# One change to a fp32 transformer block on TensorE: a half-size first x block, a partial sum in the norm chain, transposes and fill products at the turns, and the SSD product moved into the next group's x job

## The chip, the cores and the metric

The kernel runs on one core of one Trainium2 chip. The metric is device time in microseconds from start to end of the program, on that core; the kernel before was run three times (2749.87, 2750.21 and 2752.62 us; median 2750.21). A further execution was recorded by the hardware profiler, and all rows below come from it.

## What is computed

One layer of a streaming encoder block in fp32, for 256 tokens of width 2048:

```
h = x + 0.5 * post(FFN1(pre(x)))                    # SwiGLU, inner width 5632; pre and post are RMS norms
u = pre(h);  proj = u @ w_in                        # pool | z | x,B,C | dt | two gates
merged = sigmoid(g_A) * poolmix(...) @ w_pool_out + sigmoid(g_B) * ssd(...) @ w_ssd_out
h = h + post(merged @ w_mix_out)
h = h + post(cross_attention(pre(h), mem))          # 4 heads, 256 memory tokens
h = h + 0.5 * post(FFN2(pre(h)))
```

The SSD branch has 8 groups of 8 heads. Per group: x and z are projected from u, x goes through a causal convolution of 4 taps and SiLU, a decay matrix per head, exp(differences of the cumulated dt * A), is multiplied by C times B (masked), and the head's output is that matrix times x * dt, plus a skip term; then it is gated by SiLU(z) and normed over the group's 512 columns.

## The kernel before

**Chunks.** Every weight matrix is read in chunks of 256 rows by 512 columns (512 KB). A job is one block of 512 output columns: 8 chunks for a contraction over 2048 ("gate", "up", "x", "z", "pin0" and so on), 22 for "down". There are 953 chunks in the order in which the jobs are planned. SyncE loads each chunk into `raw`, a ring of four. To keep fp32 precision with the fast fp32r matmul, every operand is split in a high and a low part: ScalarE copies `raw` to `wh` (line 991), VectorE subtracts to get `wl` (line 1385), and TensorE does three products per tile pair, `wh*ul`, `wh*uh` and `wl*uh`. Both other engines work three chunks ahead (`AHEAD`): `to(n)` means "split chunks until the one of number n + 2 is done". In the code of VectorE and ScalarE other work stands between such steps, in a fixed order written out by hand; each engine runs its list in order. A job in token form (`token_chunks`, lines 634 to 636) has 12 matmuls of 512 columns per chunk, one in feature form (`feature_chunks`, lines 668 to 671) 24 of 256 columns. Jobs alternate between two PSUM slots `J`; a second PSUM tensor `A` with two areas takes transposes and small products.

**Start.** SyncE loads the identity, then alternately a block of 512 columns of x and a weight chunk. TensorE turns x block 0 and block 1 (8 transposes each, line 685), then runs chunks 0 and 1, turns blocks 2 and 3 and the gain rows, and goes on. ScalarE makes `uh` (line 1048) and VectorE `ul` (line 1486) of each turned block, between the first chunks' splits; after the last block ScalarE squares all of x (line 1062) before it splits chunk 6. The row norm itself is applied behind the products, in SiLU.

**Norms behind a job by halves** (n = 1 before "pin0", n = 3 before the second FFN, n = 4 at the end). The last three chunks of the job ahead are run for the first 128 tokens (row tile 0) and then for the other 128 (`last_by_half`). ScalarE squares each half (line 1039) and takes a root (line 1010), VectorE adds up four partial sums (line 1458), scales (line 1459), multiplies by the gain row (line 1462), inverts the root (line 1470) and adds to the residual `res` in four blocks of 512 columns (line 1433): all of tile 0, then all of tile 1. TensorE turns the updated blocks (line 707): blocks 0 and 1 of both tiles, two chunks of the next job, then blocks 2 and 3.

**The SSD group loop.** A group has an x job in feature form and a z job in token form, 16 chunks, with c0 the first. VectorE's list in group i, before the change:

```
to(c0+1): finish_gate(i-1)       to(c0+3): finish_var(i-1)       to(c0+4): finish_scale(i-1)
to(c0+7): 24 operations into E (lines 1827 to 1829), seg_ready
to(c0+8): conv_in (x_in, line 1627), 4 + 3 * 4 operations of the taps (xc), one chunk split after each of the last three fours
to(c0+12): E = E * cbm (line 1838)
to(c0+14): Xdt, yb (lines 1842, 1844)        to(c0+16)
```

`finish_gate` adds the SSD product to `yb` and multiplies by SiLU(z); ScalarE then squares it, `finish_var` scales the sums, ScalarE takes the root, and `finish_scale` inverts it, scales `yb` and transposes it by 32 blocks into `y_turn`, which GpSimd moves to `yn` with 16 transfers (line 524). `y_turn` and `zs`, the SiLU(z) of the next group, share memory: ScalarE's `finish_z` waits until the move is done. TensorE turns the convolved x after z chunk 4 (line 879) and runs the SSD product, short matmuls of 64 columns (lines 888 to 890), after the z job. GpSimd also loads `csb`, the cumulated sums of the next group.

Of the kernel before, what the change touches and what calls it, by code (L numbers as in the profile page):

```python
# [19 lines left out]
ALU = mybir.AluOpType  # L20
# [6 lines left out]
P = 128  # L27
# [14 lines left out]
def hybrid_block(nc, x, mem, ffn1_pre_g, ffn1_w1, ffn1_w3, ffn1_w2, ffn1_post_g, mix_pre_g, w_in, b_gate,  # L42
# [118 lines left out]

    with ExitStack() as ctx:
# [84 lines left out]
        ssum, sv, ss, sr, ssq_res, sr_u, sr_q = (stat[:, 8 + 2 * i:10 + 2 * i] for i in range(7))  # L247

        HALF_NORMS = (1, 3, 4)
        UPDATES = {1: NJ * T, 2: NJ * T, 3: NJ * T, 4: 2 * T}  # L250
# [42 lines left out]
        x_loaded = [sem(f"x_loaded{q}") for q in range(4)]  # L293
        first_row_loaded = sem("first_row_loaded")
# [112 lines left out]
        def _(sp):  # L407
            sp.dma_start(ident[:], identity).then_inc(ident_loaded, 16)

# [87 lines left out]
            for n in range(2 * T):  # L497

                t, c = n // 2, slice(n % 2 * D // 2, (n % 2 + 1) * D // 2)
                sp.wait_ge(res_ready, updates_before(4) + n + 1)  # L500
                sp.dma_start(out[0, t * P:(t + 1) * P, c], res[:, t, c]).then_inc(stored, 16)
            sp.wait_ge(stored, 16 * 2 * T)
# [3 lines left out]
        def _(pool):  # L506
# [38 lines left out]

            for n, g in enumerate((mix_pre_g, xattn_pre_g, ffn2_pre_g, mem_norm_g, pool_scale)):
                pool.dma_start(rows[(n + 1) * KD:(n + 2) * KD, 0, :], g[0].rearrange("(b p) -> b p", p=P)).then_inc(rows_loaded, 16)
# [59 lines left out]
        def _(pe):  # L607
# [71 lines left out]

            def turn(k, src):  # L680
# [17 lines left out]
            def turn_halves(n, qs):  # L698

                for t in range(T):  # L700
                    for q in qs:
                        pe.wait_ge(res_ready, updates_before(n) + NJ * t + q + 1)
                        if t == 0:
                            claim_area(q % 2, (f"pre{n}", q))
                        for m in range(M):
                            c = slice(q * NCOL + m * P, q * NCOL + (m + 1) * P)
                            tr = nc.tensor.transpose(area(q % 2)[:, m, t * P:(t + 1) * P], res[:, t, c], ident[:])
                        if t == T - 1:
                            tr.then_inc(t_ready[q % 2], 1)
# [17 lines left out]
            def ffn(f):  # L727
# [6 lines left out]
                def pair(i=None):  # L734
# [3 lines left out]
                    if i is None and f == 1:  # L738
                        turn_halves(n, (0, 1))
                    before = pre_wait(n) if i is None else None  # L740
                    token_chunks(("gate", f, 0), uh, ul, range(0, 2), CD - 1, i, 2 * CD, before)
                    if i is None:
                        (turn_res if f == 0 else turn_halves)(n, (2, 3))
                        if f == 0:
                            turn_rows()
                    token_chunks(("gate", f, 0), uh, ul, range(2, CD), CD - 1, i, 2 * CD, before)
# [36 lines left out]
            turn_halves(1, (0, 1))  # L783
            feature_chunks("pin0", uh, ul, range(0, 2), CD - 1, before=pre_wait(1))
            turn_halves(1, (2, 3))
            feature_chunks("pin0", uh, ul, range(2, 7), CD - 1, before=pre_wait(1))
# [72 lines left out]

            def group(i=None):  # L860
                chunk[0] = first(("x", 0))
                per = 2 * CD
                claim(("x", 0), i)
                if i is None:
                    feature_chunks(("x", 0), uh, ul, range(0, 5), CD - 1, i, per)
# [3 lines left out]
                else:  # L869
                    feature_chunks(("x", 0), uh, ul, range(0, 6), CD - 1, i, per)  # L870
                feature_chunks(("x", 0), uh, ul, range(6, CD), CD - 1, i, per)
                claim(("z", 0), i)
                token_chunks(("z", 0), uh, ul, range(0, 5), CD - 1, i, per)
# [7 lines left out]
                token_chunks(("z", 0), uh, ul, range(5, CD), CD - 1, i, per)  # L881

                pe.wait_ge(w_ready, lin(1, i, 1))
                pe.wait_ge(xdt_ready, lin(1, i, 1))
                claim_area(1, ("Y", 0), i)
                for h in range(HPG):
                    c = slice(h * HEAD_DIM, (h + 1) * HEAD_DIM)
                    nc.tensor.matmul(A[:, 1, 0, c], E[:, h, 0:P], Xdt[:, 0, c], start=True, stop=True)  # L888
                    nc.tensor.matmul(A[:, 1, 1, c], E[:, h, P:2 * P], Xdt[:, 0, c], start=True, stop=False)  # L889
                    mm = nc.tensor.matmul(A[:, 1, 1, c], E[:, h, 2 * P:3 * P], Xdt[:, 1, c], start=False, stop=True)  # L890
                mm.then_inc(t_ready[1], 1)
# [5 lines left out]
            for j in range(NJ):  # L897
                claim(("gate_b", j))
                token_chunks(("gate_b", j), uh, ul, range(CD), CD - 1)
# [77 lines left out]
        def _(act):  # L977
            at_chunk = [0]
            act.dma_start(rows[0:KD, 0, :], ffn1_pre_g[0].rearrange("(b p) -> b p", p=P)).then_inc(first_row_loaded, 16)
# [48 lines left out]
            def last_squares(name):  # L1028
# [987 lines left out]
```

## Time and profile before

| | us |
|---|---|
| median of three runs | 2750.21 |
| the profiled execution | 2751.63 |
| its span, first to last instruction | 2750.0 |
| TensorE busy | 2719.7 |
| VectorE busy | 1633.9 |
| ScalarE busy | 1288.3 |
| GpSimd busy | 346.4 |

The span is what the engines' rows cover. "Busy" of TensorE includes overlap of pipelined matmuls, so a busy engine can still be slower than it could be. "Granted clock" is a share of TensorE's full 2.4 GHz. In a timeline row "x4" means that four instructions of a kind are merged; the brackets give the idle time of the engine before the row and what ended it. In the chain of waits a row is a piece of the chain that ended last.

### The profile page before, as it was taken

The numbers are of one execution on the slowest core, as the hardware profiler recorded it, in microseconds if no ns is written. First come the engines' busy times: TensorE is split into PE (matmuls) and PEld (weight loads), VectorE is DVE, ScalarE is ACT, GpSimd is POOL, SyncE is SP. The second block draws the span as 40 slices with busy tenths as digits, with TensorE's granted clock in tenths as the row PEclk, the third lists the DMA queues.
The fourth block names the chain that finished last, engine by engine and source line by source line (L and its number), as shares of the span: only waits on it lengthen the run. The fifth ranks groups of instructions, "written<-read, shape, count | busy, mean of one in ns | idle before, by whom it ended". The sixth has DMA issues, their size and how long they took to land.

```text
span 2750.0 us, 39291 instructions
## 1 busy us (share of the span) xinstructions
PE 2719.7 (99%) x13990; PEld 2331.4 (85%) x13990; DVE 1633.9 (59%) x1912; ACT 1288.3 (47%) x1442; POOL 346.4 (13%) x619
## 2 busy tenths in 40 slices
PE   8999999999999999999999999999999999999998
PEld 7888888888899889989989888888978888888887
DVE  5555555444577556787887765566565555554444
ACT  5444444444454544455555564445654444444443
POOL 1121212000000000011311201223002122120000
PEclk9999999999999999999999999999999999999999
DMA  7777767666566665566666666677457676676554
GB/s 223 210 206 201 211 199 210 196 198 198 164 183 192 206 200 181 171 195 189 190 198 184 191 204 200 202 232 228 164 162 209 201 205 206 205 210 199 196 197 160
DMA packets 286209, 541.46 MB, mean 197 GB/s; under 512 B 27456, under 2 KB 27840, under 8 KB 285856
## 3 DMA queue, kind: packets, MB, share of 16 engines
q1 hardware_dynamic: 263104, 504.07, 59.7%
q0 software_dynamic: 22976, 36.07, 4.8%
q8 instruction: 64, 1.05, 0.1%
q14 instruction: 33, 0.27, 0.0%
q10 hardware_dynamic: 32, 0.01, 0.0%
HBM read 519.53 MB, written 2.16 MB: 190 GB/s over the span
## 4 chain that ended last, share of the span: by engine, by line
PE 94%; DVE 4%; ACT 1%; issue 1%; DMA 1%; DVEq 0%; SPq 0%; ACTq 0%
PE J L634 25%; PE J L636 25%; PE J L635 25%; PE J L668 5%; PE J L671 5%; PE J L670 5%; DVE wl L1385 1%; PE A L890 1%; PE A L889 1%; PE A L888 1%; ACT wh L991 0%; DVE E L1828 0%; DMA raw<-in_w_mix_out_dram 0%; DVE E L1829 0%; PE A L685 0%
## 5 line engine op out<-in xcount | busy, mean ns | idle before, releaser
L1385 DVE TENSOR_TENSOR wl<-raw,wh 128x1024 fp32r<-128x1024 f32 x950 | 1155.3, 1223 | 977.7 <-ACT wh L991 971.1
L991 ACT ACTIVATE wh<-raw 128x1024 fp32r<-128x1024 f32 x950 | 1004.0, 1060 | 1269.4 <-PE J L636 1017.0
L634 PE MATMUL J<-wh,ul 128*128 128x512 f32 x2048 | 801.9, 392 | 7.7 <-DVE wl L1385 4.9
L635 PE MATMUL J<-wh,uh 128*128 128x512 f32 x2048 | 798.9, 390 | 0.0
L636 PE MATMUL J<-wl,uh 128*128 128x512 f32 x2048 | 798.8, 390 | 0.0
L634 PEld LDWEIGHTS J<-wh,ul 128*128 128x128 f32 x2048 | 385.7, 188 | 94.1 <-issue 12.7
L636 PEld LDWEIGHTS J<-wl,uh 128*128 128x128 f32 x2048 | 385.6, 188 | 80.7
L635 PEld LDWEIGHTS J<-wh,uh 128*128 128x128 f32 x2048 | 385.8, 188 | 79.0
L668 PE MATMUL J<-ul,wh 128*128 128x256 f32 x1088 | 310.5, 285 | 2.0 <-DVE ul L1486 2.0
L671 PE MATMUL J<-uh,wl 128*128 128x256 f32 x1088 | 308.8, 284 | 0.0
L670 PE MATMUL J<-uh,wh 128*128 128x256 f32 x1088 | 308.8, 284 | 0.0
L517 POOL DMA_DIRECT2D hraw<-turned x320 | 173.2, 550 | 752.9 <-DVE turned L1527 746.5
L634 PE MATMUL J<-wh,hidl 128*128 128x512 f32 x680 | 264.7, 389 | 0.0
L636 PE MATMUL J<-wl,hidh 128*128 128x512 f32 x680 | 264.5, 389 | 0.0
L635 PE MATMUL J<-wh,hidh 128*128 128x512 f32 x680 | 264.5, 389 | 0.0
L668 PEld LDWEIGHTS J<-ul,wh 128*128 128x128 f32 x1088 | 209.8, 193 | 2.5 <-DVE ul L1486 2.2
L670 PEld LDWEIGHTS J<-uh,wh 128*128 128x128 f32 x1088 | 209.8, 193 | 0.1
L671 PEld LDWEIGHTS J<-uh,wl 128*128 128x128 f32 x1088 | 209.7, 193 | 0.0
L635 PEld LDWEIGHTS J<-wh,hidh 128*128 128x128 f32 x680 | 127.7, 188 | 26.6
L634 PEld LDWEIGHTS J<-wh,hidl 128*128 128x128 f32 x680 | 127.7, 188 | 26.4
L636 PEld LDWEIGHTS J<-wl,hidh 128*128 128x128 f32 x680 | 127.7, 188 | 26.3
L524 POOL DMA_DIRECT2D yn<-y_turn x128 | 74.7, 592 | 284.0 <-DVE y_turn L1527 283.6
(273 smaller groups left out, 2173.6 us busy)
## 6 DMA issues: line engine op xcount, KB each, us to landing
raw<-in_ffn_w_dram SPq DMA_DIRECT2D x528, 512.0 KB, 4.4
raw<-in_w_in_dram SPq DMA_DIRECT2D x257, 512.0 KB, 3.8
raw<-in_w_ssd_out_dram SPq DMA_DIRECT2D x64, 512.0 KB, 3.6
raw<-in_w_pool_out_dram SPq DMA_DIRECT2D x32, 512.0 KB, 4.1
raw<-in_w_mix_out_dram SPq DMA_DIRECT2D x32, 512.0 KB, 6.0
hraw<-turned POOLq DMA_DIRECT2D x320, 32.0 KB, 4.0
csb<-cs_dram POOLq DMA_DIRECT2D x16, 512.0 KB, 6.3
raw<-in_pool_w_dram SPq DMA_DIRECT2D x8, 512.0 KB, 5.0
```

The source lines that it names most:

```text
L517: pool.dma_start(dst[32 * c:32 * (c + 1), :, a * 64:(a + 1) * 64], src[32 * a:32 * (a + 1), c].rearrange("p k t n -> p k (t n)")).then_inc ...
L524: pool.dma_start(dst[32 * c:32 * (c + 1)].rearrange("p k (t a n) -> p (k t) a n", t=T, n=32)[:, :, a], src[32 * a:32 * (a + 1), c].rearran ...
L634: nc.tensor.matmul(o[:, t], b, wh[:, r, kk], start=(k == 0 and kk == 0), stop=False)
L635: nc.tensor.matmul(o[:, t], a, wh[:, r, kk], start=False, stop=False)
L636: mm = nc.tensor.matmul(o[:, t], a, wl[:, r, kk], start=False, stop=(k == last_k and kk == CK - 1))
L668: nc.tensor.matmul(o[:, m], h, b, start=(k == 0 and kk == 0 and m % 2 == 0), stop=False, skip_group_check=True)
L670: nc.tensor.matmul(o[:, m], h, a, start=False, stop=False, skip_group_check=True)
L671: mm = nc.tensor.matmul(o[:, m], l, a, start=False, stop=(k == last_k and kk == CK - 1), skip_group_check=True)
L888: nc.tensor.matmul(A[:, 1, 0, c], E[:, h, 0:P], Xdt[:, 0, c], start=True, stop=True)
L889: nc.tensor.matmul(A[:, 1, 1, c], E[:, h, P:2 * P], Xdt[:, 0, c], start=True, stop=False)
L991: nc.scalar.activation(wh[:, r], raw[:, r], ACT.Copy).then_inc(high, 1)
L1385: nc.vector.tensor_tensor(wl[:, r], raw[:, r], wh[:, r].bitcast(F32), ALU.subtract).then_inc(low, 1)
```

## The change

1. **x load.** SyncE loads the first 256 columns of x, chunk 0, the other 256 columns of block 0, chunk 1, block 1, chunk 2, chunk 3, block 2, chunk 4, block 3. The identity is loaded from ScalarE's queue. GpSimd's nine loads of gain and convolution rows wait for the second half block.
2. **Start on TensorE.** 16 products of a constant, 4 and 10 products of the identity are run ahead of and around the first transposes. Chunks 0 to 3 are run pass by pass (`pass_chunk`: all `high`, all `low_x`, all `low_w` matmuls), with the second half of block 0 turned after chunk 0, block 1 after chunk 1, block 2 after chunk 2, block 3 and the rows after chunk 3.
3. **Norm chain.** VectorE adds the first three partial sums ahead (`partial`); ScalarE adds the last one inside the root. Tile 0's last block is updated after tile 1's first two (n = 3), or after its gain product (n = 1); VectorE splits and TensorE turns in a changed order (`after_halves`) with 8 and 5 products of the identity between; at the end row tile 1 is stored in four parts.
4. **SSD.** The product of group i - 1 is run after chunk 4 of group i's x job (and of the first "gate_b" job), and VectorE's and ScalarE's pieces move with it. The move of `yn` is awaited block by block.

The core of the diff, in the order of this list (VectorE's `post_halves` and `group`, then ScalarE's `group`, stand last):

```diff
         def _(act):
             at_chunk = [0]
+            act.dma_start(ident[:], identity).then_inc(ident_loaded, 16)
...
         def _(sp):
-            sp.dma_start(ident[:], identity).then_inc(ident_loaded, 16)
...
             def load_x(k):
-                if k < 4:
-                    c = slice(k * NCOL, (k + 1) * NCOL)
-                    sp.dma_start(res[:, :, c], x[0].rearrange("(t p) d -> p t d", p=P)[:, :, c]).then_inc(x_loaded[k], 16)
+                xs = x[0].rearrange("(t p) d -> p t d", p=P)
+                if k == 0:
+                    c = slice(0, NCOL // 2)
+                    sp.dma_start(res[:, :, c], xs[:, :, c]).then_inc(x_first, 16)
+                elif k in (1, 2, 4, 5):
+                    q = {1: 0, 2: 1, 4: 2, 5: 3}[k]
+                    c = slice(q * NCOL + (NCOL // 2 if q == 0 else 0), (q + 1) * NCOL)
+                    sp.dma_start(res[:, :, c], xs[:, :, c]).then_inc(x_loaded[q], 16)
...
+            def after_halves(name, n, feature=False):
+                idle = J[:, slot(name), 1, 0:P]
+                turn_half(n, 0, 0)
+                turn_half(n, 0, 1)
+                fill(idle, ident, 8)
+                turn_half(n, 1, 0)
+                fill(idle, ident, 5)
+                pass_chunk(name, n, 0, W_FIRST, feature, after_first=lambda: turn_half(n, 1, 1))
+                pass_chunk(name, n, 1, X_FIRST, feature)
+                for q in (2, 3):
+                    for t in range(T):
+                        turn_half(n, t, q)
+                pass_chunk(name, n, 2, X_FIRST, feature)
+                pass_chunk(name, n, 3, X_FIRST, feature)
...
+                    if i is None and f == 0:
+                        pass_chunk(("gate", f, 0), n, 0, X_FIRST)
+                        turn_x_half(1)
+                        pass_chunk(("gate", f, 0), n, 1, X_FIRST)
+                        turn_res(n, (1,))
+                        pass_chunk(("gate", f, 0), n, 2, X_FIRST)
+                        turn_res(n, (2,))
+                        pass_chunk(("gate", f, 0), n, 3, X_FIRST)
+                        turn_res(n, (3,))
+                        turn_rows()
...
+            pe.wait_ge(fill_ready, 1)
+            fill(J[:, 1, 1, 0:P], ones, 16)
             pe.wait_ge(ident_loaded, 16)
-            turn_res(0, (0,))
             pe.wait_ge(first_row_loaded, 16)
             nc.tensor.transpose(J[:, 0, 0, 0:KD], rows[0:KD, 0, :], ident[0:KD, 0:KD]).then_inc(cols_ready, 1)
-            turn_res(0, (1,))
+            fill(J[:, 1, 1, 0:P], ident, 4)
+            turn_x_half(0)
+            fill(J[:, 1, 1, 0:P], ident, 10)
...
+                for t in range(T):
+                    dve.wait_ge(half_squares, T * HALF_NORMS.index(n) + t + 1)
...
+                    elif t == 0:
+                        inverse(t)
+                        for q in range(NJ - 1):
+                            quarter(0, q)
+                        gain(t)
+                        for q in range(NJ - 1, T0_FIRST[n]):
+                            quarter(0, q)
+                    else:
+                        inverse(t)
+                        quarter(1, 0)
+                        quarter(1, 1)
+                        lows(0)
+                        advance()
+                        for q in range(T0_FIRST[n], NJ):
+                            quarter(0, q)
+                        quarter(1, 2)
+                        gain(t)
+                        lows(1)
+                        advance()
+                        quarter(1, 3)
...
                 else:
                     to(c0 + 1, i, per)
-                    finish_gate(0, i - 1)
-                    to(c0 + 3, i, per)
-                    finish_var(0, i - 1)
-                    to(c0 + 4, i, per)
-                    finish_scale(0, i - 1)
+                    scale_x(0, i - 1)
+                    to(c0 + 2, i, per)
+                    weigh(slice(HPG // 2, HPG), 0, i - 1).then_inc(w_ready, 1)
+                    to(c0 + 6, i, per)
+                    finish_gate(0, i - 1)
...
                 l.then_inc(seg_ready, 1)
                 to(c0 + CD, i, per)
-                conv(("x", 0), xc, 0, i, per, M)
-                to(c0 + CD + 4, i, per)
-                dve.wait_ge(exp_ready, lin(1, i, 1))
-                nc.vector.tensor_tensor(E[:], E[:], c.to_broadcast([P, HPG, 3 * P]), ALU.mult).then_inc(w_ready, 1)
+                if i is not None:
+                    finish_var(0, i - 1)
+                conv_in(("x", 0), i, per)
+                if i is not None:
+                    finish_scale(0, i - 1)
+                conv_taps(("x", 0), xc, 0, i, per, M)
                 to(c0 + CD + 6, i, per)
+                weigh(slice(0, HPG // 2), 0, i)
...
                 to(c0 + CD, i, per)
                 if i is not None:
                     root(g_root + 1, i - 1)
...
                 nc.scalar.activation(E[:], E[:], ACT.Exp).then_inc(exp_ready, 1)
-                to(c0 + CD + 4, i, per)
+                to(c0 + CD + 6, i, per)
                 conv_silu(("x", 0), xc[:], xc_silu, i)
-                to(c0 + CD + 6, i, per)
+                to(c0 + 2 * CD, i, per)
```

`scale_x` holds the two operations that make `Xdt` and `yb`, `weigh` half of `E` times `cbm`.

## Rows read from the trace of the kernel before

**Rows 1.** The page, part 1: busy time of each engine.
```profile
PE 2719.7 (99%) x13990; PEld 2331.4 (85%) x13990; DVE 1633.9 (59%) x1912; ACT 1288.3 (47%) x1442; POOL 346.4 (13%) x619
```

**Rows 2.** Waits of TensorE: total us, times, longest us.
```profile
PE A L685 <- DMA res<-in_x_dram: 8.0, 2, 6.5
PE J L634 <- DVE wl L1385: 4.9, 9, 1.0
```

**Rows 3.** Busy time by stretch, 17 to 728 us: PE, PEld, DVE, ACT, POOL; clock.
```profile
17.00:728.00 711.00, 711.00 (x3152) 589.12 (x3150) 367.04 (x338) 313.53 (x332) 88.74 (x164) 1.00 0.68 202
```

**Rows 4.** Timeline of the start: TensorE, then ScalarE (start, us, operation).
```profile
12.92 0.76 PE L634 MATMUL J<-wh,ul 128*128 128x512 f32 x1 [0.82 <-issue]
...
16.89 0.43 PE L634 MATMUL J<-wh,ul 128*128 128x512 f32 x1
...
9.90 1.55 ACT L1048 ACTIVATE uh<-A,cols 128x256 fp32r<-128x256 f32 x4
...
26.20 1.96 ACT L1062 ACTIVATE F<-res 128x2048 f32<-128x2048 f32 x1
...
30.48 2.94 ACT L991 ACTIVATE wh<-raw 128x1024 fp32r<-128x1024 f32 x3
...
39.33 1.27 ACT L1090 ACTIVATE silu_g<-J,stat 128x512 f32<-128x512 f32 x2 [0.30 <-PE J L636]
```

**Rows 5.** Chain of waits around norm 1 (start, us, what).
```profile
736.64 0.70 ACT J L1039 x2
...
738.54 0.76 DVE res L1433
...
742.62 0.58 PE J L668
...
750.74 1.75 PE A L707 x16
...
766.88 0.43 PE A L790 x2
```

**Rows 6.** Timeline around norm 3: TensorE.
```profile
2014.20 1.97 PE L707 MATMUL A<-ident,res 128*128 128x128 f32 x8 [2.56 <-DVE res L1433]
2017.94 0.80 PE L634 MATMUL J<-wh,ul 128*128 128x512 f32 x1 [1.77 <-DVE ul L1486]
...
2039.38 0.47 PE L634 MATMUL J<-wh,ul 128*128 128x512 f32 x1 [0.18 <-DVE wl L1385]
```

**Rows 7.** Busy time and clock (PEclk) by stretch: norms and group loop.
```profile
740.50:741.00 0.50, 0.17 (x2) 0.00 (x0) 0.20 (x2) 0.50 (x3) 0.00 (x0) 0.60 0.31 90
...
2013.00:2014.00 1.00, 0.00 (x0) 0.00 (x0) 0.87 (x3) 1.00 (x2) 0.00 (x0) 0.89 0.02 8
...
1319.00:1555.00 236.00, 233.34 (x1517) 210.92 (x1516) 192.41 (x313) 127.32 (x132) 46.91 (x76) 1.00 0.63 188
```

**Rows 8.** Timeline of a group of the SSD loop: VectorE, TensorE, GpSimd.
```profile
1210.44 1.23 DVE L1385 TENSOR_TENSOR wl<-raw,wh 128x1024 fp32r<-128x1024 f32 x1 [1.65 <-ACT wh L991]
...
1222.89 1.23 DVE L1385 TENSOR_TENSOR wl<-raw,wh 128x1024 fp32r<-128x1024 f32 x1
...
1244.57 1.22 DVE L1771 TENSOR_TENSOR yb<-A,yb 128x1024 f32<-128x1024 f32 x1 [1.71 <-PE A L890]
...
1255.49 0.16 DVE L1782 RECIPROCAL stat<-stat 128x2 f32<-128x2 f32 x1
...
1257.83 1.18 DVE L1385 TENSOR_TENSOR wl<-raw,wh 128x1024 fp32r<-128x1024 f32 x1
...
1214.91 0.40 PE L634 MATMUL J<-wh,ul 128*128 128x512 f32 x1
...
1224.27 0.47 PE L634 MATMUL J<-wh,ul 128*128 128x512 f32 x1 [1.00 <-DVE wl L1385]
...
1239.07 0.33 PE L888 MATMUL A<-Xdt,E 128*128 128x64 f32 x2
...
1205.66 9.36 POOL L524 DMA_DIRECT2D yn<-y_turn  x16 [38.59 <-DVE y_turn L1527]
```

More of the change, by code:

```diff
@@ L737, in pair @@
                     n = {0: 0, 1: 3}[f]
-                    if i is None and f == 1:
-                        turn_halves(n, (0, 1))
                     before = pre_wait(n) if i is None else None
[L741 to L746, printed above, removed]
+                    if i is None and f == 0:
[8 more added lines that the diff above has]
+                        turn_rows()
+                    elif i is None:
+                        after_halves(("gate", f, 0), n)
+                    done_ks = 0 if i is not None else 4
+                    token_chunks(("gate", f, 0), uh, ul, range(done_ks, CD), CD - 1, i, 2 * CD, before)
                     if i is None and f == 0:
@@ L782, in _ @@
             claim("pin0")
[L783 to L786, printed above, removed]
+            after_halves("pin0", 1, feature=True)
+            feature_chunks("pin0", uh, ul, range(4, 7), CD - 1, before=pre_wait(1))
             pe.wait_ge(normed, 2)
@@ L858, in _, with ssd @@
             feature_job("C1")
+            def ssd(i=None):
+                pe.wait_ge(w_ready, lin(GROUPS, i, 1) if i is None else i)
+                pe.wait_ge(xdt_ready, lin(GROUPS, i, 1) if i is None else i)
+                pe.wait_ge(t_moved[1], use(1, ("Y", GROUPS - 1)) - 1 if i is None else lin(use(1, ("Y", 0)) - 2, i, 1))
+                for h in range(HPG):
+                    c = slice(h * HEAD_DIM, (h + 1) * HEAD_DIM)
+                    nc.tensor.matmul(A[:, 1, 0, c], E[:, h, 0:P], Xdt[:, 0, c], start=True, stop=True)
+                    nc.tensor.matmul(A[:, 1, 1, c], E[:, h, P:2 * P], Xdt[:, 0, c], start=True, stop=False)
+                    mm = nc.tensor.matmul(A[:, 1, 1, c], E[:, h, 2 * P:3 * P], Xdt[:, 1, c], start=False, stop=True)
+                mm.then_inc(t_ready[1], 1)
             def group(i=None):
@@ L880, in group @@
                 tr.then_inc(t_ready[0], 1)
[L881 to L891, printed above, removed]
+                token_chunks(("z", 0), uh, ul, range(7, CD), CD - 1, i, per)
             group()
@@ L1502, in pre_norm_behind @@
                 if n == 0:
-                    for q in range(2):
-                        first_splits(q)
-                        pre_low(n, q)
+                    pre_low(n, 0, range(0, 2))
+                    first_splits(0)
+                    pre_low(n, 0, range(2, M))
+                    first_splits(1)
+                    pre_low(n, 1)
                     first_splits(2)
@@ L1582, in _ @@
             ffn(0)
-            post_halves(1, ("down", 0, NJ - 1), 0.5, between=lambda q: pre_low(1, q))
+            post_halves(1, ("down", 0, NJ - 1), 0.5, lows=lambda q: pre_low(1, q))
             nc.vector.memset(ones[:], 1.0)
```

245 lines of the change are left out of this document (168 added, 77 removed).

## The prediction

> **What bounds the kernel now.** I read the page first: TensorE is busy for 2719.7 of 2750.0 us [rows 1], so a change can win only its idle time, its time at half clock, or fewer instructions; this one keeps the arithmetic. Then TensorE's waits [rows 2]: 8.0 us for x at the start and 4.9 us for `wl`, one time in each pass of the group loop. From 17 to 728 us there is no idle at all: 3152 matmuls in 711.00 us, so 0.2256 us each and 2.71 us for a chunk of 12 [rows 3]. What is left lies in four places, read as timelines: the start [rows 4], the norm before "pin0" [rows 5], the norm before the second FFN [rows 6] and the SSD group loop [rows 8]. The last view carries the most weight: it shows what precedes the one wait of each group.
>
> **Base.** The profiled execution took 2751.63 us with a span of 2750.0; the median of the runs is 2750.21. I sum changes against the profile and put them on the median.
>
> **The start.** Now the first chunk begins at 12.92, late and at half clock (full from 16.89), but afterwards TensorE never idles, and the first gate job ends where SiLU begins, 39.3 [rows 4]. After: 30 tiny matmuls fill the wait. Eight transposes at half clock take 1.97 us [rows 6], 0.21 each start to start; if the engine starts at 1.4 (assumed), 16 fills end at 4.8, the row transpose and 4 fills at 5.9, four half-block transposes at 6.8. The x half lands somewhere between 1.4 and 6.5 (the full block today, TensorE's longest wait for it [rows 2]); below 5.9 it does not matter. ScalarE then makes two `uh` (0.8) and `wh` 0 (1.0; three take 2.94) [rows 4], to 8.8. Chunk 0 starts at 8.9, 4 us earlier than now, and at full clock ends at 11.7.
>
> From there the new order costs. The second half is turned only behind chunk 0 (to 12.3); ScalarE makes `uh` 2, 3 and then `wh` 1 (1.8 us), so chunk 1 starts at 14.3: 2.0 us idle. x block 1 is turned only behind chunk 1 (to 18.0); ScalarE makes four `uh` (1.55) and then `wh` 2 (1.0), so chunk 2 starts at 20.7: 2.7 us idle. Chunks 2 and 3 and the turns behind them run to 28.3. The last block is turned at 28.0, so its `uh` end at 29.6, `wh` 5 at 30.7, and the two squares with the root (26.20 to 30.48 now, 4.3 us) let `wh` 6 start at 34.9 against 30.48 now. Chunk 5 waits 0.8 us and chunk 6 2.5 us for `wl`; chunk 7 ends near 42.8 against 39.2. **Start: +3.6 us**, between -4 (if ScalarE's queue did not hold up the turns, the 4 us of the earlier start stay won) and +7 (if the clock falls in the 2.7 us gap). I take +3.6: every wait in it is an engine's own order. Moved DMAs: `ident` goes to ScalarE's queue ahead of the gain row (one issue, behind the fills); GpSimd's nine row loads queue behind the wait for x block 0 (about 8), a half us of issue each, needed at 27.9; the last x block is issued behind `w` 4, which waits for `wl` 0 (about 10), and is needed at 27. All at nothing. If rows came after 28, every us would count.
>
> **Norm 1.** Now the second row tile is turned behind its first update, from 739.3, the first chunk starts at 742.62, and by the matmul of `diag`, 766.88, seven chunks are done [rows 5]. Added: a reduce and two scalings ahead of the last squares, under the last matmuls. Removed behind each square: a reduce, a scaling, and the gain product's place ahead of the reciprocal. The square ends at 737.3; root and reciprocal (0.2 us each) now end in 738.54, then in 737.9. An update takes 0.76, so the second tile's blocks are ready at 738.6 and 739.3 against 739.3 and 740. Turn, two `uh`, first pass: `uh` from 739.4, chunk 0 at 740.35. That is 2.3 us earlier, with the q1 turn inside the chunk, and without half clock: now the clock falls at 740.6 [rows 7], while the 13 fills leave gaps of 0.7 us only. A feature chunk is 2.88 us (752.5 to 766.88 are five); chunks 0 and 1 with the q1 turn end at 746.5. The block (1, 3) is updated after `lows(1)` and one `wl`, at 748.0, so turns end at 748.5 (1.0 us of wait, new). Five more chunks end at 762.95; `wh` 6, behind the squares, is ready at 758.3 and `wl` 6 at 759.5, 0.5 us before its use. **-3.9 us**, between -5 and -1 (without the clock's part).
>
> **Norm 3.** The same for token chunks. Now the second tile's work waits for VectorE's four first-tile updates, turns at 2014.20, chunk 0 at 2017.94, then at half clock (0.80 us for the first matmul), and chunk 6 starts at 2039.38 [rows 6, 7], so the job ends at 2044.8. After: only three first-tile updates come first, 0.68 for the product, reciprocal at 2011.7, turn at 2012.7, chunk 0 at 2014.3; chunk 1 ends at 2020.2; block (1, 3) comes at 2022.6 (1.2 us of wait); six chunks from 2023.15 end at 2039.5. **-5.3 us**, between -6.5 and -2.
>
> **The end.** The last updates are four for two, at best as fast; the reduce and the scaling behind the last square go, and the last store is half as large. **-0.2**, between -0.5 and +0.3.
>
> **The SSD loop.** The 48 short matmuls are moved and not removed: they start at 1239.07, VectorE takes their result at 1244.57 [rows 8], and TensorE has no wait among its rows for their inputs. So moving them gains nothing by itself. VectorE's order changes. With z starting at 1214.91 (its fourth chunk is the one that waits), `wl` 9 comes at 1210.44, bound to `wh` 9 and so to x chunk 5; then 24 `E`, `wl` 10, `x_in`, four taps, four taps, and `wl` 11 at 1222.89, in which VectorE idles only 0.4 us. TensorE needs `wl` 11 about 1223.1 and starts at 1224.27: 1.2 us lost per group, seven times (group 0 alike). The change takes out of that stretch nothing; `E` times `cbm`, `Xdt` and `yb` (some 5.8 us in all) stood behind it. It puts in `finish_var` (0.1) and `finish_scale`, which from reciprocal to next instruction runs 1255.49 to 1257.83, 2.34 us. `finish_gate` (2.45) moves to c0 + 6, under the 5.3 us of short matmuls, done 0.2 us before chunk 5 is, so `wl` 9 is no earlier. `wl` 11 is 2.44 us later, the wait 3.6 us. **7 x 2.44 = +17.1 us**, between 0 (if the stretch began earlier) and +23 (3.3 each). Else in the loop: ScalarE's root waits behind `wl` 10 with `Exp` and three `wh` queued behind it; `Exp` ends 7 us into z and `wh` 11 at 8, VectorE asks for it at 10.3: covered. GpSimd's `yn` move starts 6.4 us into z and takes 9.4 us to issue [rows 8], with the last landing perhaps 13 to 14; its end is awaited by ScalarE's `finish_z` 26 us into z, 6 us of slack; if it took twice as long each group would pay 7. The `E` product's second half, `Xdt` and `yb` (4.1 us) in the next x job end 5 us before the short matmuls. After the loop everything has a chunk or more of slack.
>
> **The clock in the loop.** The clock fell to 1.2 GHz at 740.6 and at 2013.9; before each fall TensorE had idled but for eight or some transposes [rows 5 to 7]. In the loop, idle times of 1.0 us never lower it [rows 7]. The new 3.4 us of idle lie between the two, nearer the first. At the start a rise took dense matmuls from 12.92 to 16.89, 4.0 us [rows 4], at 0.43 us each instead of 0.23: 1.9 us lost. I take three falls in seven groups: **+6 us**, between 0 and +20. The Trainium skill's TensorE: Matmul & The Clock Gate ("What's actually happening") says the clock is lowered only after a whole idle window; by it these gaps, with dense matmuls on both sides, would almost never lower it and the sum would be 6 us smaller.
>
> **Sum.** 3.6 - 3.9 - 5.3 - 0.2 + 17.1 + 6 = +17.3; on the median 2767.5, rounded down to **2767.0**.
>
> **Rivals.**
> (a) The same without falls of the clock in the loop: +11.3, 2761.5. For it: only gaps that held a few transposes or nothing, and were longer or began with slower work, have lowered it so far.
> (b) The other side: VectorE's stretch starts early enough, or `finish_scale` hides, so that the loop's wait does not grow. Place: between `x_in` and the first taps. The loop then costs 0 and the edges decide: -5.8, 2744.4; 2736 if today's 1.2 us go as well. It decides as soon as the growth per group is under 5.8 / 7 = 0.8 us. Against it: 0.4 us of idle in the stretch, and its start hangs on x chunk 5, which the change leaves where it is relative to z.
> (c) The clock falls in every group and in the start's gap, or the `yn` move is late too: +21 to +29, 2771 to 2779.
> (d) The half block brings nothing because it lands as late as the whole one: the start +0.7 more. Inside the range of each.
>
> **Chances.** Forecast 0.42, (a) 0.28, (b) 0.16, (c) 0.09, and 0.05 for the edges and the loop near zero together. A measurement here tells 0.2%, 5.5 us, from no change. Slower by more: 0.79 (forecast, (a), (c)); faster by more: (b) where its -5.8 or -14 hold, 0.13; within: 0.08. The range takes the forecast and (a) with their edges' bounds and most of (c): 2753 to 2778.
>
> **What would show it.** TensorE's wait of `J` for `wl` at about 3.4 us, once per group, total near 24 us, with `yb` and `y_turn` between `x_in` and `xc` on VectorE; in the start, waits for `wh` of 2.0 and 2.7 us and the first SiLU near 43; first chunk near 9; chunk 0 of "pin0" 4 us after the last FFN matmul at full clock; granted clock below 1.00 in some groups. It would be wrong if the group's period stayed near 52 us instead of 54.6, or the first SiLU came before 39.

## The result and the profile after

The changed kernel takes **2768.11 us** (median, 2766.0 to 2771.38), the kernel before 2751.80 us beside it (2749.87 to 2754.55): the ratio is 1.0061 with a 95% interval of 1.0049 to 1.0072. It is slower by 16.3 us; 2767.0 was forecast, and a change of +17.3 on a median of 2750.21, which became 2751.80 with two more runs. The profiled execution has a span of 2766.6 us against 2750.0, so the spans differ by 16.6. The page, part 1, and under it TensorE's costliest group of part 5:

```profile
PE 2730.8 (99%) x14102; PEld 2343.3 (85%) x14102; DVE 1633.1 (59%) x1920; ACT 1287.9 (47%) x1442; POOL 345.2 (12%) x619
...
L660 PE MATMUL J<-wh,ul 128*128 128x512 f32 x2016 | 789.5, 392 | 22.0 <-DVE wl L1505 21.9
```

TensorE is busy 11.1 us longer than in [rows 1], though it gained only 112 records. The new matmuls are the constant products (fills) at the turns, and the same matmuls take longer where the clock is low. The waits of TensorE (total us, times, longest) say where the idle time is:

```profile
PE J L660 <- DVE wl L1505: 21.9, 11, 2.7
PE J L737 <- ACT wh L1104: 4.5, 2, 2.6
PE J L709 <- DVE ones L1737: 1.2, 1, 1.2
PE A L771 <- DVE res L1553: 0.7, 1, 0.7
```

The 8.0 us for x [rows 2] are gone, and 4.5 us for `wh` at the start came in their place. The wait for `wl` grew from 4.9 to 21.9 us, with 18.4 of it in seven times in the loop, where it was 4.3 before, and 2.7 in two chunks at the start. To see what each part of the change did, I took the same operation in both traces and compared its start, in order of time:

```
mark (TensorE)                           before      after    part        its share
turn of hidden behind the first job      501.53     508.28    start          +6.7
first turn of norm 1                     736.44     743.18
diag matmul behind norm 1                766.71     769.84    norm 1         -3.6
first turn of merged, behind the loop   1826.45    1848.90    loop          +19.3
first turn of norm 3                    2010.36    2032.84
last matmul                             2742.02    2759.23    norm 3         -5.3
end of the span                          2750.0     2766.6    end            -0.6
```

The shares make +16.6 with rounding, the difference of the spans. What follows goes through them in this order.

**The start**, TensorE (start, duration, operation, idle time before it):

```profile
1.19 5.53 PE L709 MATMUL J<-ones 128*128 128x128 f32 x32 [1.19 <-DVE ones L1737]
...
10.40 1.17 PE L737 MATMUL J<-wh,uh 128*128 128x512 f32 x4
...
15.72 1.23 PE L737 MATMUL J<-wh,uh 128*128 128x512 f32 x4 [1.87 <-ACT wh L1104]
...
22.27 2.08 PE L737 MATMUL J<-wh,uh 128*128 128x512 f32 x4 [2.60 <-ACT wh L1104]
24.14 1.60 PE L737 MATMUL J<-wh,ul 128*128 128x512 f32 x4
25.59 1.08 PE L737 MATMUL J<-wl,uh 128*128 128x512 f32 x4
```

The first chunk starts at 10.40 instead of 12.92 [rows 4] and at full clock, but chunks 1 and 2 each wait for their `wh`. Chunk 2 then runs at half clock for its first pass and most of its second (2.08 and 1.60 us where chunk 1 has 1.23 and 1.09). ScalarE's first SiLU shows what the job has lost: 46.31 against 39.33 [rows 4].

```profile
19.71 1.57 ACT L1161 ACTIVATE uh<-A,cols 128x256 fp32r<-128x256 f32 x4 [4.04 <-PE A L751]
21.15 1.07 ACT L1104 ACTIVATE wh<-raw 128x1024 fp32r<-128x1024 f32 x1
...
46.31 1.26 ACT L1212 ACTIVATE silu_g<-J,stat 128x512 f32<-128x512 f32 x2
```

ScalarE stood idle 4.04 us until TensorE, which had chunk 1 to do first, turned the next block. Then it split that block and the weights while TensorE stood idle. The two engines take turns instead of overlapping.

The +6.7 is one execution's. Six of the experiments below (e1, e3, e4, e7, e8, e9) have the same start, and their turn of hidden lies between 506.52 (e3) and 509.63 (e1), so between +5.0 and +8.1. In e3 the 16 fills took 5.24 us, chunk 0 came at 10.11 and the clock did not fall behind it; in e1 they took 6.72 us, chunk 0 came at 11.59 and the clock fell.

**Norm 3** (norm 1 has the same form), TensorE:

```profile
2032.84 1.04 PE L771 MATMUL A<-ident,res 128*128 128x128 f32 x8
2033.72 1.95 PE L709 MATMUL J<-ident 128*128 128x128 f32 x16
...
2037.15 1.16 PE L737 MATMUL J<-wh,uh 128*128 128x512 f32 x4
...
2045.30 0.66 PE L771 MATMUL A<-ident,res 128*128 128x128 f32 x4 [0.65 <-DVE res L1553]
```

From the first turn to chunk 0 it is 4.31 us, against 7.58 before (2010.36 in the table to 2017.94, [rows 6]). The chunk runs at full clock: its first four matmuls take 1.16 us, where the first one alone took 0.80.

**The loop**, the chain of waits of one group (start, us, what):

```profile
1330.74 1.14 DVE wl L1505
...
1331.95 1.14 DVE x_in L1786
...
1333.40 0.89 DVE yb L1943 x2
...
1335.18 0.37 issue
1335.55 1.38 DVE xc L1800 x4
```

It ends in a `wl` at 1338.86 and a matmul of TensorE at 1340.24, after 2.60 us of idle time. The two scalings of `yb` and the turn `y_turn` lie between `x_in` and `xc`. By the timelines of VectorE `xc` begins 3.7 us behind `x_in`, and 1.5 us before the change. Before, then after:

```profile
1217.43 1.21 DVE L1627 TENSOR_TENSOR x_in<-J,rbc 128x1024 f32<-128x1024 f32 x1
1218.92 2.02 DVE L1641 TENSOR_SCALAR xc<-x_in,cols 128x256 f32<-128x256 f32 x4 [0.28 <-DVE x_in L1627]
```

```profile
1213.58 1.23 DVE L1505 TENSOR_TENSOR wl<-raw,wh 128x1024 fp32r<-128x1024 f32 x1 [1.44 <-ACT wh L1092]
...
1220.63 1.21 DVE L1786 TENSOR_TENSOR x_in<-J,rbc 128x1024 f32<-128x1024 f32 x1
...
1224.32 1.37 DVE L1800 TENSOR_SCALAR xc<-x_in,cols 128x256 f32<-128x256 f32 x4
```

The `wl` at 1213.58 is the one ahead of the 24 `E`, and the matmul that waits starts at 1229.12. I call these 15.5 us the stretch.

From one turn of `xc` to the next it is 54.2 us in three groups and 55.3 to 55.7 in four; it was 52.1 on average before (1230.02 to 1542.68 in six). The longer ones are those in which the clock fell. Two pieces of 3.4 us behind the wait, one with a fall and one without (columns as in [rows 7]; the clock is the third number from the end):

```profile
1229.10:1232.50 3.40, 3.38 (x10) 2.74 (x11) 3.28 (x7) 0.00 (x0) 3.40 (x7) 0.66 0.71 196
1340.20:1343.60 3.40, 3.36 (x14) 2.60 (x15) 3.28 (x7) 0.00 (x0) 3.40 (x7) 1.00 0.73 191
```

The waits ahead of them are almost equal, 2.72 and 2.60 us. Over the loop's seven waits the clock fell four times, each time for 3.4 us at 1.2 GHz.

### The profile page after: what moved, and what is told of

It is laid out like the page before. It is cut to its first block, busy times and chain, and to the rows that moved or that the text cites. A ratio compares the mean times of both kernels' runs of the same rounds, so it can differ in the third digit from the quotient of the medians.

```text
span 2766.6 us, 39541 instructions
## 1 busy us (share of the span) xinstructions
PE 2730.8 (99%) x14102; PEld 2343.3 (85%) x14102; DVE 1633.1 (59%) x1920; ACT 1287.9 (47%) x1442; POOL 345.2 (12%) x619
## 4 chain that ended last, share of the span: by engine, by line
PE 94%; DVE 4%; ACT 1%; issue 1%; DMA 0%; DVEq 0%; ACTq 0%
PE J L660 25%; PE J L662 25%; PE J L661 25%; PE J L694 5%; PE J L697 5%; PE J L696 5%; DVE wl L1505 1%; PE J L737 1%; PE A L963 1%; PE A L962 1%; PE A L961 1%; PE J L709 0%; PE J L733 0%; ACT wh L1092 0%; DMA raw<-in_w_mix_out_dram 0%
## 5 line engine op out<-in xcount | busy, mean ns | idle before, releaser
L660 PE MATMUL J<-wh,ul 128*128 128x512 f32 x2016 | 789.5, 392 | 22.0 <-DVE wl L1505 21.9
L661 PE MATMUL J<-wh,uh 128*128 128x512 f32 x2016 | 786.8, 390 | 0.0
L662 PE MATMUL J<-wl,uh 128*128 128x512 f32 x2016 | 786.8, 390 | 0.0
L660 PEld LDWEIGHTS J<-wh,ul 128*128 128x128 f32 x2016 | 380.0, 188 | 106.3 <-ACT wh L1092 21.8
L662 PEld LDWEIGHTS J<-wl,uh 128*128 128x128 f32 x2016 | 379.8, 188 | 79.5
L694 PE MATMUL J<-ul,wh 128*128 128x256 f32 x1056 | 300.2, 284 | 0.0
L697 PE MATMUL J<-uh,wl 128*128 128x256 f32 x1056 | 298.8, 283 | 0.0
L696 PE MATMUL J<-uh,wh 128*128 128x256 f32 x1056 | 298.8, 283 | 0.0
L694 PEld LDWEIGHTS J<-ul,wh 128*128 128x128 f32 x1056 | 202.6, 192 | 0.5
L696 PEld LDWEIGHTS J<-uh,wh 128*128 128x128 f32 x1056 | 202.6, 192 | 0.3
L697 PEld LDWEIGHTS J<-uh,wl 128*128 128x128 f32 x1056 | 202.6, 192 | 0.0
```

The lines of the kernel that those rows point to most:

```text
L660: nc.tensor.matmul(o[:, t], b, wh[:, r, kk], start=(k == 0 and kk == 0), stop=False)
L661: nc.tensor.matmul(o[:, t], a, wh[:, r, kk], start=False, stop=False)
L662: mm = nc.tensor.matmul(o[:, t], a, wl[:, r, kk], start=False, stop=(k == last_k and kk == CK - 1))
L694: nc.tensor.matmul(o[:, m], h, b, start=(k == 0 and kk == 0 and m % 2 == 0), stop=False, skip_group_check=True)
L696: nc.tensor.matmul(o[:, m], h, a, start=False, stop=False, skip_group_check=True)
L697: mm = nc.tensor.matmul(o[:, m], l, a, start=False, stop=(k == last_k and kk == CK - 1), skip_group_check=True)
```

## The experiments

The kernel before took 2752.50 us beside e1 to e8 (13 runs, 2751.04 to 2754.55) and 2751.61 beside e9 and e10 (15 runs, 2749.47 to 2753.42). In the traces I read the mean period of the loop from the turns of `xc`. Each of e2 to e8 is one run; their differences are to be held against the 3.5 us over which the 13 runs of the kernel before spread.

**e1: the change without its loop.** All hunks of the diff stay, but the 48 short matmuls stand behind z again and the finish of `y` in front of the 24 `E`, as before. From TensorE's part:

```
-                    ssd(i)
-                    feature_chunks(("x", 0), uh, ul, range(5, 6), CD - 1, i, per)
+                    feature_chunks(("x", 0), uh, ul, range(0, 6), CD - 1, i, per)
```

> The changed kernel with its group loop put back as it was; start and norms stay changed. Theory (VectorE's order in the loop costs 2.1 us a group, and 1.2 us for each fall of the clock, 19.3 us by the marks of the two traces): the loop's period returns from 54.2 or 55.4 to 52.1 us, TensorE's waits for wl in it to at most 1.0 us, no fall of the clock in it, time 2768.1 - 19.3 = 2748.8 us (ratio to the kernel before 0.9989). Rival (the loop is only where time lost at the norms or the start shows up): the loop would keep a period over 53 us and the time would stay above 2755.

2749.68 us (2747.09 to 2750.8), ratio 0.9988 with an interval of 0.9978 to 0.9997. The period is 52.2 us and the clock in the loop is 1.00. The other parts of the change together win 2.8 us by the medians, as their marks said (6.7 - 3.6 - 5.3 - 0.6); in the profiled execution of e1, the slowest of its ten runs, it is 0.9 us, because its start is +8.1. The loop alone turned that into a loss.

**e2: the loop alone.** The reverse: the kernel before with only the loop's hunks.

> The kernel before with the changed group loop alone. Theory: the mirror of the run above, 2751.8 + 19.3 = 2771 us, between 2766.5 (no fall of the clock) and 2775 (a fall in each of seven groups); waits for wl of 2.7 us, seven times. Rival (the loop costs only together with the changed start or norms): 2752.

2772.87 us, one run: +20.4, with a period of 55.1 and four falls of the clock in the loop, the first of them twice as long (6.8 us). Together, e1 and e2 give -2.8 + 20.4 = +17.6, and the whole change +16.3: the parts add up to about 1 us, so none of them causes or hides much of another.

**e3: the stretch 0.8 us shorter.** This leaves out the two scalings of `yb` in groups 0 to 6, so what they computed is missing from the result.

```
-                for t in range(T):
-                    l = nc.vector.tensor_scalar(yb[:, t], yb[:, t], sr[:, t:t + 1], None, ALU.mult)
-                l.then_inc(y_normed, 1)
+                if i is None:
+                    ...
+                else:
+                    dve.sem_inc(y_normed, 1)
```

> The changed kernel; in the loop the two scalings of yb by the inverse root (0.44 us each) are left out, so groups 0 to 6 are not normed. Theory (every us that VectorE works between x_in and the first taps is a us of TensorE's wait): the wait falls from 2.7 to 1.8 us, the period from 54.2 to 53.3, 6.2 us in seven groups, and with less idle time the clock falls in 0 to 2 groups instead of 4 (2.4 to 4.8 us more): 2757 to 2760. Rival (the place of the SSD product in the x job costs, not VectorE's list): 2768, the period unchanged.

2756.04 us, the period 53.4 or 53.5 in every group. The wait shrank from 2.6 to 1.8 or 1.9 us, and the clock fell in no group. The waits of TensorE in the loop (1200 to 1570 us), the changed kernel and then e3:

```profile
PE J L660 <- DVE wl L1505: 18.4, 7, 2.7
```

```profile
PE J L660 <- DVE wl L1505: 12.8, 7, 1.9
```

The time lies 1 us below the range that I expected. The start of this execution was 1.8 us shorter than the changed kernel's (506.52 against 508.28), which has nothing to do with the edit.

**e4: the stretch 0.8 us longer.** Two more scalings, with `zs` as their output, ahead of the two.

```
+                if i is not None:
+                    for t in range(T):
+                        nc.vector.tensor_scalar(zs[:, t], yb[:, t], sr[:, t:t + 1], None, ALU.mult)
```

> The changed kernel; in the loop the two scalings of yb are run a second time into a spare tile (0.9 us more). Theory: the wait grows from 2.7 to 3.6 us, 6.2 us in seven groups, and the clock falls in 5 to 7 groups (1.2 to 3.6 us more): 2775.5 to 2778. Rival (VectorE's list is not what the loop waits for): 2768.

2778.88 us, 0.9 above the range that I expected. The same view of e4:

```profile
PE J L660 <- DVE wl L1505: 23.8, 7, 3.4
```

The period is 56.2 to 56.4 where the clock fell for 3.4 us, 57.6 where it fell for 6.8, and 55.0 in the one group of seven where it did not fall. So from e3 over the changed kernel to e4 the wait goes 1.8, 2.6, 3.4 with the length of the stretch, and the falls 0, 4, 6. The whole stretch, from the `wl` ahead of the 24 `E` to the matmul that waits, is 13.2 to 13.8 us before the change, 14.6 or 14.7 in e3, 15.4 or 15.5 in the changed kernel and 16.2 in e4, and in every group of the four the wait is the stretch less 12.8 us. These 12.8 us are what VectorE has; what it takes beyond them TensorE waits for. Both terms that I forecast for the loop are shown here: VectorE's stretch sets the wait one for one, and the clock is an extra on top that comes more often with a longer wait.

**e5 and e6: another order at the start.** Both are e1 with the second half of x block 0 turned behind the first, five fills fewer, and each further block turned one chunk earlier; e6 also starts the split of chunk 6's weights ahead of the squares.

```
+            turn_x_half(1)
-            fill(J[:, 1, 1, 0:P], ident, 10)
+            fill(J[:, 1, 1, 0:P], ident, 5)
...
                         pass_chunk(("gate", f, 0), n, 0, X_FIRST)
-                        turn_x_half(1)
-                        pass_chunk(("gate", f, 0), n, 1, X_FIRST)
                         turn_res(n, (1,))
-                        pass_chunk(("gate", f, 0), n, 2, X_FIRST)
+                        pass_chunk(("gate", f, 0), n, 1, X_FIRST)
...
```

> As e1_loop_as_before (old loop, changed norms), with the start's order changed: x's second half is turned ahead of chunk 0 in place of five of the ten fills, block 1 behind chunk 0, block 2 behind chunk 1, block 3 behind chunk 2. Theory (in the changed start TensorE waits for ScalarE because each block is turned one chunk too late; the row of waits for wh, 4.5 us, the 2.7 us of waits for wl behind it and the half clock of 3.4 us go): the first gate job ends near 36.5 instead of 45.8 us, time 2749.7 - 9.3 = 2740.4 us. Rival (x has not landed so early, so the waits for wh turn into waits for x): the gate job ends above 43 and the time stays above 2747.

> As e5_start_turns_early, and ScalarE and VectorE split chunk 6 before the squares of x and the root. Theory: chunk 6 waits for wl 0.5 to 1 us at most in e5, so this gains 0 to 1 us: 2739.5 to 2740.5. Rival (the squares still set the start, as they did in the changed kernel with 1.9 us): it gains 2 us or more against e5, 2738.

2742.99 and 2742.45 us: 9.5 and 10.1 us under the kernel before and 6.7 and 7.2 under e1. The 0.5 between the two is less than single runs can tell. TensorE in e6, from chunk 0 on:

```profile
11.65 1.16 PE L737 MATMUL J<-wh,uh 128*128 128x512 f32 x4 [0.43 <-issue]
...
15.26 1.17 PE L737 MATMUL J<-wh,uh 128*128 128x512 f32 x4
...
18.87 1.17 PE L737 MATMUL J<-wh,uh 128*128 128x512 f32 x4
```

Chunk 0 starts no later than in e1 (11.65 against 11.59; 10.40 in the changed kernel, whose fills were over sooner), nothing waits behind it any more, and the clock does not fall; the first SiLU comes at 37.13. The turn of hidden is at 499.34 against 509.63 in e1, 10.3 us earlier. Of these, 1.9 are given back behind the loop: one load of `w_mix_out` took 11.91 us there (10.06 in e1), its chunk came late, and TensorE waited up to 2.2 us for it, in e5 up to 2.4. The spans differ by the 8.4 that are left (2749.1 and 2740.7). This late load is most of the 2 to 3 us by which both lie above what I expected.

**e7: the norms without fills.** e1 without the two groups of constant products in `after_halves`.

```
                 turn_half(n, 0, 1)
-                fill(idle, ident, 8)
                 turn_half(n, 1, 0)
-                fill(idle, ident, 5)
```

> As e1_loop_as_before, without the 8 and 5 fill products in the two norms by halves. Theory A (the fills keep the clock up; the gain of the norms is half the reordering and half the clock): the clock falls at one or both norms and 1.2 to 3 us each are lost, 2752 to 2755. Theory B (the reordering alone leaves gaps too short for a fall): no fall, and since the fills end before the turned blocks are ready, the same time within 0.7 us: 2749.7.

2750.41 us, 0.7 above e1's median and within its runs. TensorE at norm 1 (idle time in brackets):

```profile
746.60 0.66 PE L771 MATMUL A<-ident,res 128*128 128x128 f32 x4 [1.34 <-DVE res L1547]
748.27 1.19 PE L733 MATMUL J<-uh,wh 128*128 128x256 f32 x8 [1.02 <-ACT uh L1153]
```

Two gaps of 1.3 and 1.0 us did not lower the clock, nor did the 1.6 and 1.0 us at norm 3. In the new order of the norm the fills do nothing for the time; what wins it is the rest, the order and the partial sum, which no run separates.

**e8: the scalings behind the taps.** The changed kernel, with `finish_scale` after the first convolution taps instead of before them.

```
+                conv_taps(("x", 0), xc, 0, i, per, M)
                 if i is not None:
                     finish_scale(0, i - 1)
-                conv_taps(("x", 0), xc, 0, i, per, M)
```

> The changed kernel with finish_scale moved from between x_in and the taps to behind the taps. Theory (the wait for wl is VectorE's list; but the move of yn then starts some 10 us later and ScalarE's finish_z, which needs it done, waits): the waits for wl 11 fall to 1.0 us and the clock falls vanish, 19.3 us less, while finish_z comes 5 to 7 us late and the fourth x chunk waits 1 to 2.5 us for its wl, 7 to 17 us back: 2756 to 2766. Rival (the yn move has slack enough): 2749.

2780.39 us: slower than the changed kernel, where I had expected it to be faster. The chain of waits says why (start, us, what):

```profile
1234.01 0.89 DVE yb L1943 x2
...
1236.53 8.62 POOL yn L549 x15
1245.15 5.17 DMA yn<-y_turn
...
1251.04 0.68 ACT zs L1335
1251.72 0.95 ACT wh L1092
...
1256.32 1.24 DVE wl L1505
1257.69 0.36 PE J L694
```

The wait in z did shrink, to 1.00 us. But `y_turn` now ends near 1236 instead of 1224, GpSimd needs 8.6 us to issue its 16 moves, and the last of them lands at 1250.3. ScalarE's `zs` waits for that (6.98 us idle), with the splits of the weights queued behind it, and TensorE then waits in the next x job:

```profile
PE J L694 <- DVE wl L1505: 11.6, 9, 2.1
PE J L660 <- DVE wl L1505: 9.5, 13, 1.0
```

In the changed kernel the same `zs` at 1245.68 is released by TensorE and not by the moves. This is the mechanism of my rival (c), the late `yn` move, and I had put 6 us of slack on it in the prediction. A delay of 12 us uses that up and more. The expectation named this wait and took 7 to 17 us for it, which was much too little: from the `diag` matmul to the first turn of merged it is 10.8 us more than in the changed kernel, where I had expected 2 to 12 less. One reason is that the clock went on falling. It fell at 1310.5, 1368.5, 1481.2 and 1593.8, each time within 1.4 us behind the end of one of the new waits, of 1.9 to 2.5 us. The rest of the difference is not worked out.

**e9: the stretch begins earlier, in the changed kernel.** The first 12 of the 24 `E` tiles may be written one chunk earlier; the work stays the same.

```
-                else:
-                    to(c0 + 7, i, per)
...
-                    if i is None and h == HPG // 2 - 1:
-                        to(c0 + 7)
+                    if h == HPG // 2 - 1:
+                        to(c0 + 7, i, per)
```

> The changed kernel; the one edit is that VectorE may write the first 12 of a group's 24 E tiles one chunk earlier (from chunk 6 of the x job), in the time in which it stood idle ahead of the low product of wl. In the profile of the changed kernel VectorE stood idle 1.44 us at that place (1213.58, behind ACT wh) and then had no idle time until the low product that TensorE waited 2.72 us for (1229.12). If the unbroken stretch of VectorE work sets that wait, it begins up to 1.44 us earlier, the wait falls to about 1.3 us, the four falls of the clock in the loop (1.2 us each, behind gaps of 2.6 to 2.7 us) go too, and the time falls by 7 x 1.4 + 4 x 1.2 = 14.6 us to about 2753.5 us, wl waits of TensorE from 21.9 to about 12 us. If the wait comes from the order of the taps and low products alone, or from the transfers of the weights, nothing moves: 2768 us.

2753.14 us (2752.06 to 2753.64, ten runs), ratio to the kernel before 1.0006 with an interval of 0.9996 to 1.0015. The period is 52.7, and the clock stays up in every group. This one edit of an order takes back 15.0 us of what the change lost. It shows that the place of VectorE's work, not its amount, sets the time: by the waits it took 1.5 us out of each group, about as much as VectorE had stood idle ahead of the stretch (1.44 us), and with the shorter waits the four falls went too. TensorE's waits in the loop:

```profile
PE J L660 <- DVE wl L1505: 5.4, 5, 1.1
PE J L660 <- ACT wh L1092: 2.3, 2, 1.2
```

**e10: the same edit on e6.** The norms of the change, the start of e6, and the loop as before with the halved `E`.

> The kernel of e6 (the norms of the change, its start with the turns one chunk earlier, the loop as before), with one edit: the first 12 of the 24 E tiles may be written from chunk 6 of the x job instead of chunk 7. In the profile of e6 TensorE waited for wl 4.6 us in the loop, 7 times, longest 1.0, and VectorE stood idle 1.65 us just ahead of the stretch that ends in that wait. If the stretch sets the wait, all 4.6 us go: 2742.5 - 4.6 = about 2738 us, and no wait of TensorE on wl is left in the loop. If something else sets it: 2742.5 us with the waits unchanged. The work on either engine is the same in both.

**2731.73 us** (2730.99 to 2732.15), ratio 0.9927 with an interval of 0.9913 to 0.9941: 19.9 us under the kernel before and 36.4 under the changed one. Busy time by stretch (TensorE first), e6 and then e10:

```profile
1100.00:1500.00 400.00, 395.63 (x2691) 364.03 (x2690) 319.91 (x535) 205.02 (x210) 68.72 (x110) 1.00 0.64 188
```

```profile
1100.00:1500.00 400.00, 399.87 (x2750) 372.07 (x2749) 322.12 (x537) 209.48 (x217) 68.91 (x110) 1.00 0.62 190
```

TensorE's idle time in the loop is gone. It gave 10.7 us where I expected 4.6; by the spans it is 10.2, of which 8.2 lie ahead of the first turn of merged and 2.1 behind it. The 2.1 are the late load of e6, which took 9.91 us here. The 8.2 are the loop, whose period went from 52.2 to 51.1 us. The wait rows understate a gap: the modelled end of a matmul lies 0.16 us past the start of the next one, so the gap of 0.43 us at 1217.92 in e6 cost 0.59, and the first matmul behind it 0.07 more. Over seven gaps that is 1.6 of the 3.6 us between 4.6 and 8.2. Another 1.3 lie one chunk later, where no gap is listed: in each group of e6 the next chunk's first matmul starts 0.31 to 0.35 us behind the one before it instead of 0.23, and the matmul behind it is 0.08 late again (1220.53, 1220.84 and 1221.15 in the first of the seven). The last 0.7 are open; e6 has one run only.

## Why the prediction was right

**The start, +3.6 forecast, +6.7 measured.** The mechanism held: every wait in my list is there. `wh` 1 and `wh` 2 release the first two (1.87 and 2.60 us, forecast 2.0 and 2.7), `wl` 5 and `wl` 6 the other two (0.87 and 1.87, forecast 0.8 and 2.5). Two sizes were off. I took 0.21 us for a fill, from the eight transposes at half clock in [rows 6]. A 128-column product of these is two records, and 16 of them took 5.53 us, so 0.34 us each, and chunk 0 came at 10.40 instead of 8.9: +1.5. And I counted falls of the clock for the loop alone, though I had forecast a gap of 2.7 us here: chunk 2 took 4.23 us up to the turn behind it (22.27 to 26.50) where chunk 1 took 2.92 (15.72 to 18.64), +1.3. With these the term is 6.4, and the marks show 6.7. The half block landed at 4.11, where the whole one landed at 6.40 before, so rival (d) is excluded; but with the fills as long as they were, its turn came at 7.81 and the earlier landing won nothing. No wait for a moved DMA shows. In e5 and e6, with the turns one chunk earlier, the term is -1.8 and -2.2, so the order of the turns, with the fall of the clock that followed from it, was the whole cost.

**Norm 1, -3.9 against -3.6, and norm 3, -5.3 against -5.3.** The steps held too: in norm 3 chunk 0 starts 4.31 us behind the first turn, at full clock, and the block (1, 3) is waited for 0.65 us (forecast 1.2). In norm 1 that wait of 1.0 us did not come; VectorE had the block done at 754.9, ahead of its turn. e7 corrects one reason: I ascribed the full clock to the fills, and it stays up without them.

**The end, -0.2 against -0.6.** Within the bounds.

**The loop, +17.1 against +14.6.** The place, the releaser and the count were right: one wait per group, on the `wl` behind the first taps, with `yb` and `y_turn` ahead of it. The term was 2.44 us for each group and measured 2.1 (54.2 less 52.1). I took the whole 2.34 from the reciprocal to the next instruction, and 0.1 for `finish_var`. But in the old order `xc` began 1.49 us behind `x_in`, 0.28 of it waiting for `x_in` itself, and now it begins 3.68 behind: 2.2 more and not 2.34. From there to the `wl` it is 0.25 us less on average than before, for which I have no reason. The whole stretch grew by 2.0 (13.4 to 15.4 on average), and so did the wait. The rows with the wait say 2.6 or 2.72 and not 3.6 since, besides, the wait before was 0.6 on average and not 1.2: I had read it off the first of the seven groups, which has the longest (4.3 us in seven). Rival (b), that the wait would not grow, fell with the first trace, and e3, e4 and e9 show that the wait goes with the stretch.

**The clock in the loop, +6 against +4.7.** Three falls at 1.9 us were forecast. There were four, and the rest of the loop's 19.3 us, 4.7, makes 1.2 for each (the periods say 1.3). So rival (a), with no falls, did not come, nor (c), with a fall in every group. The price was taken from the start, where the rise came after 4.0 us; here it came after 3.4, with 0.43 instead of 0.23 us for each matmul, which should lose 1.6. Where the other 0.3 to 0.4 us come back, no run separates. The rule that I quoted from the Trainium skill's TensorE: Matmul & The Clock Gate ("What's actually happening"), by which gaps like these almost never lower the clock, does not agree with the trace: it fell in four of seven.

So the total was right to 1.1 us partly by luck, because errors cancelled: the start 3.1 us too cheap, the loop with its clock 3.8 too dear. The start alone varies by 3.1 us between traces with the same code there.

## What to carry to other kernels

Before work is moved to another place, ask what it stands in front of on its engine: the scalings moved here cost 2.1 us in each group though the engine was only 59% busy, and halving one block of 24 operations gave back 15.0 us (e9) and won 10.7 more elsewhere (e10). An unbroken stretch on a helper engine matters as soon as it is longer than the lead of the buffers it feeds; here that was 12.8 us, and every 0.8 us beyond it was 0.8 us of wait (e3, e4). If a turn feeds a split that feeds the next chunk, issue the turn one chunk ahead (e6: the first SiLU is 9.2 us earlier than in the changed kernel); and after moving something back, look at what is late next (e8).

## What the runs showed of the hardware

Gaps of TensorE in the loop's z jobs, with dense matmuls on both sides, lowered the clock in no group at 1.8 to 1.9 us (e3), in four of seven at 2.6 to 2.7 (the change, and again e2), and in six of seven at 3.4 (e4). A gap's length alone does not decide. In e8, in the x jobs and behind them, four gaps of 1.88, 2.11, 2.12 and 2.47 us were each followed by a fall, and those of 1.1 to 1.5 us were not. The same 2.60 us gap at the start lowered the clock in the changed kernel and not in e3, and the 1.87 us gap ahead of it did in e1 and not in the changed kernel. What else decides, no run shows.

The fall can come before or behind the end of the gap. In the first group of the change TensorE was back at work at 1229.12, and its matmuls started 0.23 us apart up to 1230.12 and 0.43 apart from 1230.50 on; at the start the clock was low before the gap ended at 22.27 (0.55 granted from 21.8 to 22.2), and so it was ahead of 1226.42 in e2. In the loop a fall lasted 3.4 us in most cases and 6.8 us in two (e2 at 1225.8, e4 at 1286.1).
